# The final norm of a hybrid block, moved from a stage of its own into the last expert's last pass

## The reference

```
hn   = rmsnorm(x, norm_mix_g);  proj = hn @ w_in
mix  = concat(s5(proj...), mlstm(proj...))
h    = x + mix @ w_out
t    = rmsnorm(h, norm_ffn_g)
for each token the 4 best of 32 experts, gate = softmax of their scores:
  g, lin = split(t @ w_up[e] + b_up[e]);  g = min(g, 7);  lin = clip(lin, -7, 7)
  h += gate * ((g * sigmoid(1.702 g) * (lin + 1)) @ w_down[e] + b_down[e])
out  = rmsnorm(h, norm_final_g)
rmsnorm(x, g) = x * rsqrt(mean(x * x) + 1e-5) * g
```

## Time and profile before

| | |
|---|---|
| median of 3 runs | 2322.02 us (2321.19 to 2322.78) |
| the profiled execution's own time | 2317.68 us |
| its span (first to last instruction) | 2315.9 us |
| PE busy | 2154.9 us, 93% |
| DVE busy | 1621.6 us, 70% |
| ACT busy | 1211.6 us, 52% |
| POOL busy | 553.8 us, 24% |
| mean granted TensorE clock | 0.967 |
| DRAM read and written | 513.09 MB and 64.60 MB |

### The profile page before, as it was taken

How to read it: one execution, slowest core, us unless ns; L and a number is a source line. 1 busy time by engine, 2 the same in 40 slices (tenths; PEclk the granted TensorE clock), 3 DMA queues, 4 the chain that set the end, 5 groups by cost and what they waited for, 6 DMA issues and landing times. The chain is left out here.

```text
span 2315.9 us, 32381 instructions
## 1 busy us (share of the span) xinstructions
PE 2154.9 (93%) x10442; PEld 1788.5 (77%) x10443; DVE 1621.6 (70%) x1866; ACT 1211.6 (52%) x1243; POOL 553.8 (24%) x534
## 2 busy tenths in 40 slices
PE   6999986799399999999999999999999999999993
PEld 5787876488288888888888888888888888888872
DVE  4688857546775665779579775877975787686773
ACT  4422243232264554667467564757754675565663
POOL 1001121104511110413134140513511251121412
PEclk9999977999599999999999999999999999999997
DMA  6123273441595676969689795988986798787974
GB/s 178 56 82 137 79 133 110 135 150 65 211 351 187 227 235 195 320 223 379 233 296 375 269 313 188 349 293 292 365 289 203 267 369 303 225 283 257 311 238 170
DMA packets 285925, 540.89 MB, mean 234 GB/s; under 512 B 37194, under 2 KB 53690, under 8 KB 284770
## 3 DMA queue, kind: packets, MB, share of 16 engines
q1 hardware_dynamic: 260418, 490.58, 61.0%
q0 software_dynamic: 25440, 49.47, 8.3%
HBM read 513.09 MB, written 64.60 MB: 249 GB/s over the span
## 5 line engine op out<-in xcount | busy, mean ns | idle before, releaser
L2433 DVE TENSOR_TENSOR ex_w_lo<-ex_raw,ex_w_hi 128x2048 fp32r<-128x2048 f32 x408 | 926.9, 2289 | 374.7 <-ACT ex_w_hi L2326 308.1
L2326 ACT CAST ex_w_hi<-ex_raw 128x2048 fp32r<-128x2048 f32 x371 | 706.7, 1910 | 278.5 <-PE ex_ps_g L2642 99.9
L2237 POOL TENSOR_TENSOR ex_passed<-ex_ident 128x1 f32<-128x1 f32 x136 | 138.3, 1017 | 1187.0 <-ACT ex_y L2369 1154.1
L2641 PE MATMUL ex_ps_g<-ex_w_hi,ex_x_hi 128*128 128x512 f32 x784 | 307.9, 393 | 9.2 <-issue 7.2
L2641 PE MATMUL ex_ps_l<-ex_w_hi,ex_x_hi 128*128 128x512 f32 x784 | 308.6, 394 | 1.2 <-DVE ex_w_lo L2433 1.2
L2642 PE MATMUL ex_ps_g<-ex_w_lo,ex_x_hi 128*128 128x512 f32 x784 | 305.9, 390 | 0.0
L2642 PE MATMUL ex_ps_l<-ex_w_lo,ex_x_hi 128*128 128x512 f32 x784 | 305.3, 389 | 0.0
L2641 PE MATMUL ex_ps_y<-ex_w_hi,ex_h_hi 128*128 128x512 f32 x544 | 217.0, 399 | 0.6
L2645 PE MATMUL ex_ps_g<-ex_w_hi,ex_x_lo 128*128 128x512 f32 x544 | 212.6, 391 | 0.0
L2642 PE MATMUL ex_ps_y<-ex_w_lo,ex_h_hi 128*128 128x512 f32 x544 | 212.0, 390 | 0.0
L2645 PE MATMUL ex_ps_l<-ex_w_hi,ex_x_lo 128*128 128x512 f32 x544 | 212.0, 390 | 0.0
(11 more groups left out here) (468 smaller groups left out, 3704.8 us busy)
## 6 DMA issues: line engine op xcount, KB each, us to landing
ex_raw<-in_w_up_dram SPq DMA_DIRECT2D x272, 1024.0 KB, 8.6
ex_raw<-in_w_down_dram SPq DMA_DIRECT2D x136, 1024.0 KB, 7.9
st_tab<-tabs SPq DMA_DIRECT2D x8, 1408.0 KB, 6.7
pr_raw<-in_w_in_dram SPq DMA_DIRECT2D x10, 1024.0 KB, 5.4
tabs<-pr_x POOLq DMA_DIRECT2D x32, 256.0 KB, 2.3
por_raw<-in_w_out_dram SPq DMA_DIRECT2D x16, 256.0 KB, 5.7
t<-mix_sig_o SPq DMA_DIRECT2D x8, 512.0 KB, 2.6
fi_h<-h SPq DMA_DIRECT2D x8, 512.0 KB, 7.2
```

Of the source, the lines that this page charges most:

```text
L2237: pool.tensor_tensor(passed[:, :], ident[:, 0:1], ident[:, 0:1], ALU.add).then_inc(passed_done, 1)
L2326: nc.scalar.copy(w_hi[:, j % SPLIT, :, :], raw[:, j % RAW, :, :]).then_inc(hi_done, 1)
L2433: v.tensor_tensor(w_lo[:, j % SPLIT, :, :], raw[:, j % RAW, :, :], w_hi[:, j % SPLIT, :, :].bitcast(F32), ALU.subtract).then_inc(lo_done, 1)
L2641: pe.matmul(to[:, :], hi_in[:, b, kk, :], w_hi[:, s, k, :], start=first, stop=False)
```

## The change

`finish` is gone; its work is inside `experts`, in the pass of kind `LAST`.

- SP, behind that pass's 12 weight loads: load the final gain, wait for the previous scatter (`y_free`), load tiles 0 to 3 of `h3`, wait for `lo` of the pass's eighth chunk, load tiles 4 to 7 into two freed ring slots. Later it stores each scaled tile.
- ACT, between the pass's own work: `square` of tiles 0 and 1 after `hi_ahead` of chunk 10, of 2 and 3 after that of chunk 11, of 4 to 7 after the second `h_high`.
- POOL: gathers the pass's own rows of `h3` (without this pass's addition) into `x_rows`; takes the power of tiles 0 to 3, 4 and 5, 6 and 7 as three batches, each an add of eps and a power.
- DVE, behind the pass's last work: `scale` of the 8 tiles in place.
- When `y` is written: POOL adds it to `h3` as before. DVE adds `y` to the gathered rows, ACT squares them, POOL takes the power, DVE scales them, and when all tile stores have landed POOL writes these rows to `out` by an indirect DMA. SP waits for that write.
- If `most` asked for further passes, all 8 tiles would be done once more at the end (`norm_again`).
- POOL loads `most` and the last expert's `plan` ahead of the last expert's passes.
- In `project`, `square(2)` moves behind `hi(0)`, and `mean(2)` and `norm(2)` behind `lo(0)`.

```
@@ -464,7 +464,8 @@
                     turned_in(j)
                     if j == 1:
                         hi(0)
-                    if j + 2 < TT:
+                        square(2)
+                    if 1 <= j < TT - 2:
                         square(j + 2)
                     if j == 2:
                         hi(1)
@@ -642,7 +643,7 @@
                 norm(0)
                 mean(1)
                 for j in range(TT):
-                    if j + 1 < TT:
+                    if j + 1 < TT and j != 1:
                         norm(j + 1)
                     for half in range(2):
                         v.wait_ge(t_hi, 2 * j + half + 1)
@@ -652,7 +653,9 @@
                                         ALU.subtract).then_inc(t_free, 1)
                     if j == 1:
                         lo(0)
-                    if j + 2 < TT:
+                        mean(2)
+                        norm(2)
+                    if 1 <= j < TT - 2:
                         mean(j + 2)
                     if j == 2:
                         lo(1)
...
+        RAW_USED = 8
+        BATCHES = [slice(0, 4), slice(4, 6), slice(6, 8)]
+
+        def final_tile(j):
+            if j < 3:
+                return done_rows[:, j, :]
+            if j == 3:
+                return bias_rows[:, D:2 * D]
+            return raw[:, j // 2 - 2, j % 2 * 2:j % 2 * 2 + 2, :].rearrange("p a n -> p (a n)")
...
-        def more_items(eng, body):
-
-            most = eng.value_load(keep["most"][0:1, 0:1], min_val=0, max_val=T)
+        def more_items(eng, body, end=None, most=None):
+
+            if most is None:
+                most = eng.value_load(keep["most"][0:1, 0:1], min_val=0, max_val=T)
...
+                if end is not None:
+                    end()
...
+                def final_load(j):
+                    sp.dma_start(final_tile(j), h3_t[:, j, :]).then_inc(final_in[j], 16)
+
+                def final_store(j, before):
+                    sp.wait_ge(result_set, before + j + 1)
+                    sp.dma_start(out_t[:, j, :], final_tile(j)).then_inc(stored, 16)
+
+                def norm_all_but_last(n, blocks):
+                    sp.wait_ge(bias_set, 2)
+                    sp.dma_start(final_gain, p["norm_final_g"].rearrange("(a d) -> a d", a=1).to_broadcast([P, D])).then_inc(final_gain_in, 16)
+                    for b in range(PAIR):
+                        sp.wait_ge(y_free[b], n * 16 + 16)
+                    for j in range(TT):
+                        if j == 4:
+                            sp.wait_ge(lo_done, n * CHUNKS + (LOW + RAW_USED))
+                        final_load(j)
+                    for j in range(TT):
+                        final_store(j, 0)
+                    sp.wait_ge(stored, 16 * TT)
+                    sp.wait_ge(rows_out, 16 * blocks)
+                    sp.sem_inc(rows_written, 1)
...
+                    if kind is LAST:
+                        norm_all_but_last(n, blocks)
...
+                def power(i, again):
+                    part = BATCHES[i]
+                    pool.wait_ge(squared, again * TT + part.stop)
+                    pool.tensor_scalar(mean[:, part], mean[:, part], RMS_EPS, None, ALU.add).then_inc(eps_added, 1)
+                    pool.wait_ge(eps_added, 2 + i + again * len(BATCHES))
+                    pool.tensor_tensor(rstd[:, part], mean[:, part], neg_half[:, 0:part.stop - part.start], ALU.pow).then_inc(rstd_set, 1)
+
+                def add_rows(b, blocks):
+                    to = scatter_at[:, b, 0:1] if b < blocks else nowhere[:, 0:1]
+                    pool.indirect_dma_start(
+                        out=h3_dram, out_offset=bass.IndirectOffsetOnAxis(ap=to, axis=0),
+                        in_=y[:, b, :], in_offset=None, bounds_check=last_token, oob_is_err=False,
+                        compute_op=ALU.add).then_inc(y_free[b], 16)
+
+                def last_pass(n, at, turn, blocks):
+                    for b in range(PAIR):
+                        pool.wait_ge(y_free[b], n * 16 + 16)
+                    pass_on(turn)
+                    pool.tensor_copy(scatter_at[:, :, :], places[:, bass.ds(at, PAIR), :]).then_inc(scatter_set, 1)
+                    pool.wait_ge(scatter_set, n + 1)
+                    pool.wait_ge(t_full, n * FILLS + (FIRST + 2 * (blocks - 1)))
+                    for b in range(PAIR):
+                        pool.wait_ge(x_full[b], n * 16 + 16)
+                    pass_on(turn + 1)
+                    for b in range(blocks):
+                        pool.indirect_dma_start(
+                            out=x_rows[:, b, :], out_offset=None, in_=h3_dram,
+                            in_offset=bass.IndirectOffsetOnAxis(ap=scatter_at[:, b, 0:1], axis=0),
+                            bounds_check=last_token, oob_is_err=False).then_inc(back_in[b], 16)
+                    for i in range(len(BATCHES)):
+                        power(i, 0)
+                    pool.wait_ge(y_a_read, n + 2)
+                    pool.wait_ge(y_b_read, n + 2)
+                    carry_on(1)
+                    for j in range(TT):
+                        pool.wait_ge(final_in[j], 16)
+                    for b in range(blocks):
+                        pool.wait_ge(back_in[b], 16)
+                    add_rows(0, blocks)
+                    pool.wait_ge(row_squared, blocks)
+                    pool.tensor_scalar(row_mean[:, 0:blocks], row_mean[:, 0:blocks], RMS_EPS, None, ALU.add).then_inc(row_eps_added, 1)
+                    pool.wait_ge(row_eps_added, 1)
+                    pool.tensor_tensor(row_rstd[:, 0:blocks], row_mean[:, 0:blocks], neg_half[:, 0:blocks], ALU.pow).then_inc(row_rstd_set, 1)
+                    add_rows(1, blocks)
+                    pool.wait_ge(row_done, blocks)
+                    pool.wait_ge(stored, 16 * TT)
+                    for b in range(blocks):
+                        pool.indirect_dma_start(
+                            out=out_rows, out_offset=bass.IndirectOffsetOnAxis(ap=scatter_at[:, b, 0:1], axis=0),
+                            in_=x_rows[:, b, :], in_offset=None, bounds_check=last_token, oob_is_err=False).then_inc(rows_out, 16)
...
+                most = pool.value_load(keep["most"][0:1, 0:1], min_val=0, max_val=T)
+                plan = pool.value_load(keep["plan"][0:1, E - 1:E], min_val=1, max_val=8 * 2 * E + 7)
+                last = pool.snap((plan >> 3) + ((plan >> 1) & (plan & 1)))
                 last_passes(pool, one_pass)
...
-                more_items(pool, later)
-                plan = pool.value_load(keep["plan"][0:1, E - 1:E], min_val=1, max_val=8 * 2 * E + 7)
-                last = pool.snap((plan >> 3) + ((plan >> 1) & (plan & 1)))
...
+                def square(j, again):
+                    act.wait_ge(final_in[j], 32 if again else 16)
+                    if again or j:
+                        act.wait_ge(squared, again * TT + j)
+                    nc.scalar.activation(junk, final_tile(j), ACT.Square, scale=D ** -0.5,
+                                         accum_out=mean[:, j:j + 1]).then_inc(squared, 1)
+
+                def square_row(b):
+                    act.wait_ge(row_added, b + 1)
+                    act.wait_ge(squared, TT)
+                    if b:
+                        act.wait_ge(row_squared, b)
+                    nc.scalar.activation(junk, x_rows[:, b, :], ACT.Square, scale=D ** -0.5,
+                                         accum_out=row_mean[:, b:b + 1]).then_inc(row_squared, 1)
...
+                        if kind is LAST and j in (6, 7, 8):
+                            for t in range(4 if j == 8 else 2):
+                                square(2 * j - 12 + t, 0)
+                    if kind is LAST:
+                        for b in range(blocks):
+                            square_row(b)
...
+                def scale(j, again):
+                    v.wait_ge(rstd_set, again * len(BATCHES) + 1 + [j < batch.stop for batch in BATCHES].index(True))
+                    v.wait_ge(final_in[j], 32 if again else 16)
+                    v.scalar_tensor_tensor(final_tile(j), final_tile(j), rstd[:, j:j + 1], final_gain,
+                                           ALU.mult, ALU.mult).then_inc(result_set, 1)
+
+                def norm_all_but_last(n, blocks):
+                    v.wait_ge(final_gain_in, 16)
+                    for j in range(TT):
+                        scale(j, 0)
+                    v.wait_ge(y_a_read, n + 2)
+                    v.wait_ge(y_b_read, n + 2)
+                    for b in range(blocks):
+                        v.wait_ge(back_in[b], 16)
+                        v.tensor_tensor(x_rows[:, b, :], x_rows[:, b, :], y[:, b, :], ALU.add).then_inc(row_added, 1)
+                    v.wait_ge(row_rstd_set, 1)
+                    for b in range(blocks):
+                        v.scalar_tensor_tensor(x_rows[:, b, :], x_rows[:, b, :], row_rstd[:, b:b + 1], final_gain,
```

(77 more changed lines are left out.)

79 lines of the change are left out of this document (15 added, 64 removed).

## The result

The changed kernel takes 2300.4 us (median of 4 runs, 2298.9 to 2302.0) where the kernel before takes 2321.6 (4 runs, 2317.0 to 2322.8): the ratio is 0.9913, with a 95% interval of 0.9899 to 0.9927. Forecast were 2300.7 us. Its profiled execution took 2300.07 us, with a span of 2298.3. That span is 17.6 less than that of before, while the medians are 21.2 apart. The first experiments take up this gap.

A forecast was written before the change was run, and what follows sets the result against it. The prediction saw the kernel bound by the 37.4 us tail behind `y`, with PE idle in `finish`, and by PE's late start. Saving 18.1 plus 3.2, 21.3 us, from 2322.02 gave 2300.7 us, range 2296.0 to 2307.5 (8 in 10).

The forecast's parts named there:

- The front, 3.2: Projection's start: with tile 2's square out of the chain, PE starts near 18.7 instead of 21.89, 3.2 us earlier.
- Only the tail pays: Rival, projection: the front's 3.2 is absorbed by a load that doesn't move; 2303.9 us, chance 0.13.
- The last pass: Last expert pass: squares on ACT delay `h_high`, PE loses 1.2, covered afterwards; scales run from 2273.6 to 2283.9.
- 1.2 late against chunk 9: Sign, last pass on PE: chunk 10 would come about 1.2 us late relative to chunk 9.
- The powers: POOL's three power batches, 3.0 us each for batches 2 and 3, barely keep DVE's scales running; otherwise 2.6 more.
- What still follows: Tail after the scales end at 2283.9: rows' add, square, power, scale, then write and block end, finishing at 2297.8.
- last tile store lands: Tail: last scaled tile's store, issued at 2284, lands 4.2 to 6.3 later, median 2289.3.
- rows' write lands: Tail: POOL's write of gathered rows to `out` starts near 2290.0, takes 6.3, lands at 2296.3.
- landing to the span's end: Tail: after the row write SP loads `most`, 0.6, and the block ends in 0.9, at 2297.8.
- slower: Rival, whole kernel: longer code makes jumps dearer through instruction fetch; above 2326.7 us, chance 0.04.
- POOL is late: Rival, tail: DRAIN waits for the row write (+3.1), power batches stall scales (+2.6), or both; 2303 to 2307, chance 0.13.
- The sum: Whole kernel: 18.1 at the tail plus 3.2 at the front, 21.3 us saved, giving 2300.7 us.

The follow-up runs named there:

- The first experiments: Kernel before with only the projection's new order: 2317.4 us, ratio 0.9987; changed kernel with the projection's old order: 2304.6 us, ratio 0.9937.
- front_only: Kernel before with only the projection's new order (tile 2's square, mean and norm behind the first weight piece): 2317.4 us, ratio 0.9987 to before.
- squares_late: Changed kernel with all eight final-norm squares behind the last pass's second `h_high` on ACT: 2306.6 us, ratio 0.9923 to before; experts' stage 1690.6.
- eight_powers: Changed kernel with the final norm's powers in eight one-tile batches instead of three: 2301.1 us, ratio 0.9916 to before; experts' stage 1686.3.
- no_add: Changed kernel with POOL's two additions to `h3` only where further items follow, so skipped here: 2297.4 us, ratio 0.9900 to before; experts' stage 1685.4.
- no_add_sp_last: Changed kernel without POOL's `h3` additions, SP's `most` load and jump ahead of its final waits: 2301.2 us, ratio 0.9909 to before; experts' stage 1682.5.
- pool_waits: Changed kernel with POOL also waiting for the rows' write before its queue's end: 2305.8 us, ratio 0.9946 to before; experts' stage 1689.7.

## Why the prediction was right, and where it was not

**The front, 3.2.** It held in place and size: PE started at 18.60 to 18.67 against 18.7 forecast, and front_only's medians are 3.2 apart. By the project block the new order alone gives 3.6 to 4.7, save in the one execution with the low clock. "Only the tail pays" falls.

**The last pass.** On before's clock, forecast against measured: `h_high` 2272.0 and 2272.3, PE's chunk 10 2273.3 and 2273.8, `y` finished 2279.7 and 2280.3, first scale 2273.6 and 2274.0, last scale ended 2283.9 and 2283.7, the rows scaled 2288.5 and 2288.3. The sum came out, but its first term had the wrong cause in part. PE's loss, 1.2 forecast and 1.6 measured, was put down to the squares alone; squares_late shows that they make 0.5 of it. In the changed kernel PE stands only 0.40 for `h_low` ahead of chunk 10, so the sign "1.2 late against chunk 9" did not come. The rest is there whenever ACT idles some 4.6 us at the pass's start, in all nine profiled kernels with the new tail (4.58 to 4.79; front_only 1.12). No run separates the two, so that this idle is the cause is likely and not shown. Nor does a run show what the idle is. ACT's last instruction ahead of it ends at 2242.23, 0.26 behind a branch, and two instruction packets of 8 KB follow (2243.3 and 2244.1); but in before two come equally far behind that branch, and ACT runs on. That the loss is covered was right.

**The powers.** "Barely" was right for three batches: adds of 0.71 and 1.30 and powers of 1.60 and 1.61 beside scales, no gap. That POOL waits for a running scale agrees with the Trainium skill (SBUF — State Buffer, "SBUF: two separate sides"), 1.46 against 0.57 in eight_powers.

**What still follows.** Here two terms were off, in opposite directions, and one was missing. From the last store's issue on:

| step | forecast | measured |
|---|---|---|
| last tile store lands | 5.3 | 7.1 |
| rows' write lands | 6.3 | 3.7 |
| landing to the span's end | 0.6 + 0.9 = 1.5 | 4.2 |

The store was late because the addition of the same pass's rows runs beside it (4.8 without it, no_add; 3.7 in eight_powers, where the store comes ahead of most of the addition). The row write was priced by additions and gathers, and the plain write took less here than the fastest of these, 4.3; over all runs it took 3.4 to 4.7. The step that failed is the last: of SP's `most` and the end of the block only the load and the barrier were priced. The jump behind the load, 2.4 us here, lay under the last pass in before (5.2 there) and is now the last thing that SP does; no_add_sp_last takes load and jump away and gains 2.9. The rival "slower" had said that by the Trainium skill's rule (Runtime: NRT & Kernel Launch, "Instruction fetch mechanics") one or two such stalls at the end of the path would cost some 2 us. The measured gap agrees in size. All seven kernels with SP's jump at the end have this gap, 2.4 to 2.6 us, with an instruction packet in it (pool_waits two); the two that take the jump earlier have neither there. So code is fetched in the gap; that SP stands still for it is inferred from this. So the tail gave 16.4 (by the spans, put on one clock) to 16.8 (by the stages) for a forecast of 18.1: 1.8 and 2.7 lost, 2.6 won.

**POOL is late.** As forecast the drain did not wait for the row write's landing; it began at 2293.1, before it. Yet on before's clock it did not end "by 2295.6, under the cover of the row write" but at 2298.2: POOL's last wait was met 0.4 later than forecast, then nothing was visible on POOL for 1.9, and the drain took 3.9 and not 3.74. It ties with SP instead of lying 1.3 us below its end. pool_waits gives the price without cover: 3.7, for 3.1 named.

**The sum.** 2300.7 was met by 2300.4. Part of that is luck: 18.1 stood for 16.6, and the difference of the medians, 21.2, is made up by a front that gave more than 3.2 by the project block and by untouched stages that vary by more than what is missing. The lower bound is also added up wrongly: 2300.7 less the three terms named is 2296.6, and not 2296.0.

## What to carry to other kernels

Work moved under a running pass is paid for only where it then ends last: follow each queue to the block's end, with its load, its jump and its drain, for what was covered before by the very stretch that is taken away. A queue that has nothing left to decide should take its jump before its last wait, not behind it. Where untouched stages vary with the clock by as much as the effect, cut the execution at the block ends and compare the one stage; and where the stage has a loop whose code is the same, count from the loop's end, as squares_late needed.

## What the runs showed of the hardware

- POOL's drain at the end of the experts' block lasts 3.7 (before) to 3.9 us (pool_waits) with nothing in flight and, when it starts earlier, until 1.2 to 1.3 us after the last indirect write landed (4.5 in eight_powers, 5.1 in no_add_sp_last, 5.5 in no_add). At the ends of before's other blocks it lasts 1.1 to 4.1 us.
- A jump over skipped code, at the end of a queue, was followed by 2.4 us on SP in which only an 8 KB instruction packet moves, and by 5.2 us on SP in before, beside the weight loads. On POOL it was followed by 0.4 us, and a further 1.9 us in which nothing is visible came behind POOL's last wait.
- An indirect plain write of 128 rows to DRAM lands in 3.4 to 4.7 us; the accumulating one of the same rows took 7.6 to 9.4 beside the tile stores.
- The same block of 368 products took 78.8 to 84.2 us from one execution to the next, at a mean granted clock of 0.78 to 0.72.
